# Hybrid conv/MoE step: one block shape with 32 rows of each of two experts, gate/up one block ahead, sorted pairs of experts

## The chip, the cores and the metric

The kernel runs on one core of a Trainium2 chip. The metric is the device time of one execution in microseconds (us). A core has five engines with their own instruction streams: TensorE (PE: matmuls, and transposes against an identity), VectorE (DVE), ScalarE (ACT), GpSimd (POOL) and SyncE (SP, which here only issues DMAs and waits). They meet through semaphores: an instruction may wait until a semaphore has reached a count. `bank0` to `bank7` are the eight PSUM banks, everything else named here lies in SBUF, except `h_rows`, `x_rows` and `y_rows`, which are the profile's names for scratch tensors in DRAM.

## The reference: what is computed

One decoder layer on 576 tokens (512 of a prompt, 64 of samples) of 1024 channels, all in float32. First a gated convolution mixer (not touched by the change), then a mixture of experts:

```
t   = RMSNorm(x)                                  # 576 x 1024
grp = argmax(t @ w_coarse + b)                    # 4 groups
top 2 of the 8 fine logits of that group          # so each token goes to 2 of 32 experts
out[token] += combine * (silu(t @ w_gate[e]) * (t @ w_up[e])) @ w_down[e]
y   = RMSNorm(x + out)
```

An expert's three matrices are 1 MB each (1024x256, 1024x256, 256x1024), 3.15 MB (10^6 bytes) in all, so the 32 experts are 100 MB, and each is read once from DRAM whatever the number of its tokens. How many tokens each expert gets follows from the inputs alone. For the inputs that are timed, experts 0 to 31 get

```
13 11 106 69 | 11 73 6 153 | 25 27 36 45 | 7 14 6 6 | 1 6 7 70 | 20 66 17 29 | 67 21 28 49 | 71 27 6 59
```

rows, 1152 in all.

## The kernel before: how the work is tiled and ordered

**Routing.** For each tile of 128 tokens (`NT` = 5 tiles, the last of 64) DVE selects the two experts (`select`), PE counts ranks within the expert by triangular matmuls (`rank`, L1498), and DVE turns ranks into a block number and a row in the block. `turns()` counts the tokens of the first two tiles and moves the pair of experts (2m, 2m+1), m >= 4, that has the fewest to the end of the order. At the end DVE holds `ends` (the block at which each expert ends), PE inverts the table with a one-hot matmul (L1550), and `gidx` / `sidx` say for each block which half rows to gather and scatter. `bound` holds the ends for the engines' registers.

**Blocks.** The experts are worked on in pairs, and rows in blocks of `T` = 64. Each pair has one block that is shared: 32 rows of the first expert and 32 of the second. What an expert has over 32 rows goes in blocks of 64 of its own, the first expert's ahead of the shared block and the second's behind it. So a pair with c0 and c1 rows has 1 + ceil((c0-32)/64) + ceil((c1-32)/64) blocks (a negative term counts as 0).

**One block** on PE is gate/up (`L1572` in a block of one expert: 16 matmuls of 64 rows by 256 columns; `L1577` in a shared block: 32 of 32 rows; the profile lists each float32 matmul of this kind twice), a dummy matmul `L1584`, four transposes `L1563` of the next block's gathered tokens (`tokens`), one transpose of the hidden values `L1587`, and the down product `L1597`. Beside it ACT does silu (`L722`) and copies the down product out of PSUM (`L726`), DVE multiplies (`L1256`, `s_hid`), copies the transposed hidden values (`L1258`, `s_hidT`), scales the next tokens (`L1249`, `s_xt`) and moves the gathered rows (`L1245`, `s_mv`), and POOL gathers (`L867`) two blocks ahead and scatters (`L897`) the block that is out. All of it is in program order on each engine; nothing is scheduled by a tool.

**Weights.** There are 8 slots for experts (`NSLOT`), so 4 rounds (`it` = 0 to 3). Slots 2m and 2m+1 hold the m-th pair of a round. The first round's experts are loaded while the mixer runs. From then on SP refills the slots in order: for each expert it waits until gate/up of the last block that used the slot is done (`s_gu`), issues gate (L440) and up (L440), waits until its last down product is done (`s_down`), and issues down (L438). A slot of a first expert is free after the shared block, one of a second expert at the end of the pair. After the last weights SP issues the loads of the residual (`xf`, L534) and `g_final` (L535) into slot memory, and once all scatters have landed those of the experts' results (L543).

**The end.** The results of the two experts of a token are read back from `y_rows`, weighted and added (DVE, and PE for two tiles), normalized and written out.

Of the kernel before, what the change touches and what calls it, by code (L numbers as in the profile page):

```python
# [6 lines left out]
P = 128  # L7
KC = D // P
SEQ = 512
NS, SL = 8, 8  # L10
NTOK = SEQ + NS * SL
# [16 lines left out]
T = 64  # L28
# [6 lines left out]
NBLK = NPAIR + NE + (2 * NTOK - NE * (T // 2 + 1)) // T  # L35
# [13 lines left out]
def build_step(nc, a, out):  # L49
# [8 lines left out]
    with ctx:  # L58
# [128 lines left out]
        bound = sb("bound", [1, 2 * NE + 4 + NPAIR], i32)  # L187

        PAIRS, ODD, LASTP, ORDER = NE + 1, NE + 2, NE + 3, NE + 4
        ENDS = ORDER + NE  # L190

        BITS = 6
        assert NBLK < 1 << BITS

        eps_rms, eps_ln = small[:, 60:61], small[:, 61:62]
        carry = sb("carry", [P, 6])[:, :]
        NCON = 18 + 2 * CC
# [113 lines left out]
        iota16, groupof = col(NPAIR), col(NE)  # L311

        expert_at, pair_at = iota32, iota16
# [5 lines left out]
        ends = col(NE)  # L319
# [3 lines left out]
        evens = col(NE)  # L323


        low32, sgn, sgnq, lower = col(2 * NT), col(2 * NT), col(2 * NT), col(2 * NT)
# [11 lines left out]
        pari, pairu = rtu[:, 0:2 * NT], rtu[:, 2 * NT:4 * NT]  # L338
        counti, nbi = coli(NE), coli(NE)
        nblki, pairi, parti, rowi = coli(1), coli(1), coli(1), coli(2 * NT)  # L340

# [15 lines left out]
        early = ps[7][:, 64 + 6 * NE:64 + 7 * NE]  # L357
# [28 lines left out]
        def _(sp):  # L386
# [123 lines left out]
            def turn(it, i):  # L510
                return (sp.value_load(bound[0:1, bass.ds(it * NSLOT + (i + ORDER), 1)], min_val=0, max_val=NE - 1),
                        sp.value_load(bound[0:1, bass.ds(it * NSLOT + (i + 1 - NSLOT), 1)], min_val=1, max_val=NBLK))

# [17 lines left out]
            left = sp.value_load(bound[0:1, NE - NSLOT + 1:NE - NSLOT + 2], min_val=1, max_val=NBLK)  # L531
# [24 lines left out]
        def _(act):  # L556
# [162 lines left out]
            def block_of(q, b):  # L719

                act.wait_ge(s_gu, q * 2 + (b + 1))
                nc.scalar.activation(sg_m, ps[1][:, 0:P], ACT.Silu).then_inc(s_silu, 1)  # L722
                act.wait_ge(s_down, q * 2 + (b + 1))
                if not isinstance(q, int):
                    act.wait_ge(s_ysc[b], q * 16)
# [956 lines left out]
```

## Time and profile before

| | us |
|---|---|
| median of three executions | 526.67 (526.08 to 532.02) |
| the profiled execution, its own time | 528.73 |
| span of that execution, first to last instruction | 527.0 |
| PE busy in the span | 478.6 (91%) |
| first gate/up starts | 273.07 |
| last down product ends | 494.9 |

All moments in the text are us from the start of the span of the profiled execution. Busy time says only that an instruction was in the engine; the chain of work that ended last says which engine's work set the end, and what an engine waited for is shown behind its idle time with the group it waited on.

### The profile page before, as it was taken

The page shows a single profiled execution, that of the slowest core. Times are in us where ns is not written, and L with a number is a line of the kernel's source. Part 1 is how long each engine was busy: PE and PEld are TensorE (multiplying, and loading weights), DVE is VectorE, ACT ScalarE, POOL GpSimd, SP SyncE. Part 2 cuts the span into 40 slices and gives each one's busy share as a digit, 9 for nine tenths or more (in the row PEclk, how much of TensorE's full clock was granted, in tenths as well). Part 3 has the DMA queues.
Part 4 walks back from the last instruction along what each step waited for, and adds up shares of the span by engine and source line. Part 5 has one row for each costly group of instructions (what it writes and reads, how often), then busy time and mean ns, then how long its engine had stood idle before and what let it go on. Part 6 is the DMA issues. An engine that isn't in the chain of part 4 may idle for free.

```text
span 527.0 us, 8895 instructions
## 1 busy us (share of the span) xinstructions
PE 478.6 (91%) x3289; PEld 283.4 (54%) x3290; DVE 237.0 (45%) x513; ACT 102.1 (19%) x209; POOL 183.0 (35%) x282
## 2 busy tenths in 40 slices
PE   6999999999999999999679999989979998979784
PEld 3887777777777645555434444444434444434331
DVE  4219999999993520335742222112212221122146
ACT  5130011011112523323511111111101111110213
POOL 3010915665575800101153434443433433442100
PEclk9989999999999999999789999999999999999998
DMA  8995005200000299936769999999999999999887
GB/s 328 319 391 157 0 2 206 113 2 0 1 1 1 87 363 424 393 146 205 308 227 420 416 410 390 418 418 419 415 387 419 422 418 419 395 414 420 268 280 260
DMA packets 43992, 146.01 MB, mean 277 GB/s; under 512 B 10240, under 2 KB 18448, under 8 KB 32697
## 3 DMA queue, kind: packets, MB, share of 16 engines
q1 hardware_dynamic: 37242, 131.06, 64.7%
q0 software_dynamic: 4960, 9.45, 4.8%
q10 hardware_dynamic: 1759, 5.06, 2.5%
q8 instruction: 22, 0.36, 0.3%
q14 instruction: 9, 0.07, 0.0%
HBM read 136.83 MB, written 15.53 MB: 289 GB/s over the span
## 4 chain that ended last, share of the span: by engine, by line
PE 77%; DMA 7%; issue 6%; DVE 4%; ACT 3%; SPq 1%; POOL 1%; DVEq 0%; POOLq 0%; ACTq 0%
PE bank L1374 27%; PE bank L1577 10%; PE bank L1457 10%; PE bank L1597 9%; PE bank L1572 9%; PE bank L1367 4%; DMA region_x<-in_w_up 2%; DMA region_w<-y_rows 2%; PE bank L1587 2%; PE bank L1483 2%; DVE region_m L1256 1%; DVE region_m L1258 1%; ACT region_m L722 1%; PE bank L1523 1%; DMA y_rows<-region_m,slast 1%
## 5 line engine op out<-in xcount | busy, mean ns | idle before, releaser
L1374 PE MATMUL bank<-region_m,region_w 128*128 128x256 f32 (+1 forms) x576 | 142.3, 409 | 0.0
L1374 PEld LDWEIGHTS bank<-region_m,region_w 128*128 128x128 f32 x576 | 110.3, 192 | 30.4 <-issue 0.6
L1256 DVE TENSOR_TENSOR region_m<-region_m,bank 128x128 f32<-128x128 f32 x30 | 8.7, 288 | 160.5 <-ACT region_m L722 160.5
L1457 PE MATMUL bank<-region_w,z 128*128 128x512 f32 x128 | 56.7, 595 | 0.2 <-ACT z L647 0.2
L1015 DVE SCALAR_TENSOR_TENSOR z<-region_m,z 128x512 f32<-128x512 f32 x60 | 48.7, 812 | 0.0
L1015 DVE SCALAR_TENSOR_TENSOR region_x<-region_m,region_x 128x512 f32<-128x512 f32 x56 | 45.9, 820 | 0.0
L1597 PE MATMUL bank<-region_w,region_m 128*32 128x512 f32 x272 | 40.3, 598 | 2.8 <-DVE region_m L1258 2.8
L807 POOL TENSOR_TENSOR region_m<-region_x 128x512 f32<-128x512 f32 x4 | 20.2, 5053 | 63.6 <-ACT region_m L601 32.4
L1457 PEld LDWEIGHTS bank<-region_w,z 128*128 128x128 f32 x128 | 23.8, 190 | 28.0 <-issue 26.3
L878 POOL COPY gcol<-gidx 128x1 uint32 (+1 forms) x30 | 5.4, 181 | 95.1 <-DVE region_m L1245 95.1
L589 ACT ACTIVATE region_x<-bank 128x256 f32<-128x256 f32 (+1 forms) x40 | 14.2, 407 | 123.6 <-PE bank L1374 104.0
L867 POOL DMA_INDIRECT region_x<-h_rows,gcol x30 | 31.7, 1055 | 15.1 <-issue 15.1
L726 ACT ACTIVATE region_m<-bank 128x512 f32<-128x512 f32 x30 | 17.9, 598 | 93.8 <-PE bank L1597 93.8
L1572 PE MATMUL bank<-region_w,z 128*64 128x256 f32 x288 | 34.6, 391 | 0.3 <-issue 0.3
L897 POOL DMA_INDIRECT y_rows<-region_m,scol x28 | 29.0, 1034 | 15.1 <-issue 15.1
L371 POOL TENSOR_SCALAR region_m<-region_m 128x128 f16<-128x128 f32 x7 | 6.0, 868 | 72.6 <-DVE region_m L1149 72.6
L1577 PE MATMUL bank<-region_w,z 128*32 128x256 f32 x384 | 30.6, 389 | 0.0
L722 ACT ACTIVATE region_m<-bank 128x128 f32<-128x128 f32 x30 | 8.3, 278 | 109.6 <-PE bank L1577 65.7
L1572 PEld LDWEIGHTS bank<-region_w,z 128*64 128x64 f32 x288 | 19.5, 134 | 18.7 <-issue 7.9
L1563 PE MATMUL bank<-ident,region_m 128*128 128x128 f32 x124 | 25.2, 286 | 2.4 <-DVE region_m L1245 2.4
L1597 PE MATMUL bank<-region_m 128*32 128x512 f32 x176 | 25.0, 598 | 1.5 <-DVE region_m L1258 1.5
L824 POOL TENSOR_TENSOR region_m<-region_x 128x512 f32<-128x512 f32 x4 | 11.4, 2842 | 31.0 <-ACT region_x L589 31.0
(240 smaller groups left out, 642.8 us busy)
## 6 DMA issues: line engine op xcount, KB each, us to landing
region_w<-in_w_down SPq DMA_DIRECT2D x16, 1024.0 KB
region_w<-in_w_gate SPq DMA_DIRECT2D x12, 1024.0 KB, 16.1
region_w<-in_w_up SPq DMA_DIRECT2D x12, 1024.0 KB
region_m<-in_w_down SPq DMA_DIRECT2D x12, 1024.0 KB
region_w<-in_w_in SPq DMA_DIRECT2D x4, 2048.0 KB, 18.7
region_m<-in_w_gate SPq DMA_DIRECT2D x8, 1024.0 KB
region_m<-in_w_up SPq DMA_DIRECT2D x8, 1024.0 KB
slot<-in_w_gate SPq DMA_DIRECT2D x4, 1024.0 KB
```

Source lines behind the costliest of these rows:

```text
L726: nc.scalar.activation(yblk[b], ps[3][:, :], ACT.Copy).then_inc(s_yc, 1)
L807: pool.tensor_tensor(ub[:, c, HB:HB + SEQ], sv[:, 0:SEQ], sg[:, 0:SEQ], ALU.mult)
L867: pool.indirect_dma_start(stage[b], None, h2_half, bass.IndirectOffsetOnAxis(ap=rows, axis=0), bounds_check=2 * NTOK - 1, oob_is_err=False ...
L897: pool.indirect_dma_start(y_half, bass.IndirectOffsetOnAxis(ap=rows, axis=0), yblk[b], None, bounds_check=4 * NTOK - 1, oob_is_err=False). ...
L1015: last[j % 2] = conv(nc.vector.scalar_tensor_tensor(out=acc[j % 2], in0=ub[:, c, j:j + SEQ], scalar=wB(c, j), in1=acc[j % 2], op0=ALU.mult ...
L1367: ins = mm(ps[2 * bank + j][:, at:at + hi - lo], sec[name][:, k, 0:P], hT[:, k, lo:hi], start=(k == 0), stop=(k == KC - 1))
L1374: ins = mm(ps[2 * bank + j][:, 0:LEN[j]], sec[name][:, k, c * P:(c + 1) * P], hT[:, k, CUT[j]], start=(k == 0), stop=(k == KC - 1))
L1457: ins = mm(ps[2 * (t % 2) + j][0:n, :], z[:, k, t * P:t * P + n], w_out_sb[:, k, j * 512:(j + 1) * 512], start=(k == order[0]), stop=(k == ...
L1563: ins = tr(ps[0][:, k * P:(k + 1) * P], xrow[:, k * P:(k + 1) * P], ident[:, :])
L1572: ins = mm(ps[1][h * T:(h + 1) * T, 0:2 * P].rearrange("p (w f) -> p w f", w=2), xT[:, k, :], wgu[halves[0]][:, :, k, h, :], start=(k == 0 ...
L1577: ins = mm(ps[1][r0:r0 + H, 0:2 * P].rearrange("p (w f) -> p w f", w=2), xT[:, k, half * H:(half + 1) * H], wgu[i][:, :, k, h, :], start=( ...
L1597: ins = mm(ps[3][quarter * H:(quarter + 1) * H, :], hidT[:, c * T + r0:c * T + r0 + H], wdn[halves[quarter % 2]][:, c, h * 512:(h + 1) * 512],
```

## The change

Every block now has one shape: 32 rows of each of the two experts of a pair. A pair with c0 and c1 rows has max(1, ceil(max(c0, c1)/32)) blocks, in all of which both experts' weights are used. On PE the blocks are software-pipelined: gate/up of block g+1 stands ahead of the transpose of block g's hidden values, of the next tokens' transposes and of block g's down product; ACT and DVE follow that order, and gate/up of a block waits for the product (`s_hid`) of the one before, as both use `bank1`. The dummy matmul L1584 is gone. `turns()` now counts the tokens of the first three tiles and sorts all of experts 8 to 31 by that count, largest first; neighbours in that order are the pairs. It moves from the fourth tile's turn to the fifth's, `rank` of the third tile four steps earlier on PE. SP waits for the end of a pair for both its slots, and issues gate and up of both experts, then down of both. Its order of slots is as before, and so are the loads before the loop.

```diff
-NBLK = NPAIR + NE + (2 * NTOK - NE * (T // 2 + 1)) // T
+HT = T // 2
+NBLK = (2 * NTOK + NPAIR * HT - 1) // HT
...
             with sp.Fori(1, NE // NSLOT) as it:
-                for i in range(NSLOT - 2):
-                    reload(i, *turn(it, i), range(3))
-                ends_of = [(i, *turn(it, i)) for i in range(NSLOT - 2, NSLOT)]
-                for which in (range(2), range(2, 3)):
-                    for i, e, last in ends_of:
-                        reload(i, e, last, which)
+                for i in range(0, NSLOT, 2):
+                    last = sp.value_load(bound[0:1, bass.ds(it * (NSLOT // 2) + (i // 2 + 1 - NSLOT // 2), 1)],
+                                         min_val=1, max_val=NBLK)
+                    pair = [(i + k, turn(it, i + k)) for k in range(2)]
+                    for which in (range(2), range(2, 3)):
+                        for j, e in pair:
+                            reload(j, e, last, which)
...
             act.wait_ge(s_x1d[NT - 1], 16)
-            for b in range(2):
-                block_of(0, b)
-            with act.Fori(1, pairs) as q:
-                for b in range(2):
-                    block_of(q, b)
+            silu(0, 0)
+            silu(0, 1)
+            y_out(0, 0)
+            silu(1, 0)
+            y_out(0, 1)
+            silu(1, 1)
+            y_out(1, 0)
+            with act.Fori(1, pairs - 1) as q:
+                silu(q + 1, 0)
+                y_out(q, 1)
+                silu(q + 1, 1)
+                y_out(q + 1, 0)
...
             def turns():
...
+                for r in range(0, NE - NSLOT, 8):
+                    link(nc.vector.max(top[:, r:r + 8], key))
+                    if r < NE - NSLOT - 8:
+                        link(nc.vector.scalar_tensor_tensor(out=key, in0=key, scalar=top[:, r + 7:r + 8], in1=key,
+                                                            op0=ALU.is_lt, op1=ALU.mult))
+                link(nc.vector.tensor_copy(topi, top))
+                link(nc.vector.tensor_scalar(topi, topi, NE - 1, None, ALU.bitwise_and))
+                link(nc.vector.tensor_copy(expert_at[:, NSLOT:NE], topi))
+                marks(0, NT - 2, s_again)
+                link(pairs_of(0, NT - 2))
+                placed(0, NT - 2).then_inc(s_place, NT - 2)
...
-                pe.wait_ge(s_mv, g + 2)
-                mm(ps[5][0:32, 0:1], onesb[:, 0:32], onesb[:, 0:1], start=True, stop=True)
-                tokens(0, KC // 4)
+            def next_tokens(g):
+                pe.wait_ge(s_mv, g + 1)
+                tokens(0, KC // 2).then_inc(s_xt_ps, 1)
+
+            def turn_hidden(g):
                 pe.wait_ge(s_hid, g + 1)
                 tr(ps[2][:, 0:P], hid, ident[:, :]).then_inc(s_hT_ps, 1)
-                tokens(KC // 4, KC // 2).then_inc(s_xt_ps, 1)
...
-            def pair(it, i, first, after, end):
+            def pair(it, i, first, end):
                 for part in range(2):
-                    pe.wait_ge(s_wexp[i][part], it * 16 + 16)
-                with pe.If(after > first + 1):
-                    with pe.Fori(first, after - 1) as g:
-                        block_of(g, (i, i), it)
-                for part in range(2):
-                    pe.wait_ge(s_wexp[i + 1][part], it * 16 + 16)
-                block_of(after - 1, (i, i + 1), it)
-                with pe.If(end > after):
-                    with pe.Fori(after, end) as g:
-                        block_of(g, (i + 1, i + 1), it)
+                    for half in range(2):
+                        pe.wait_ge(s_wexp[i + half][part], it * 16 + 16)
+                gate_up(first, i)
+                if isinstance(first, int):
+                    next_tokens(1)
+                else:
+                    turn_hidden(first - 1)
+                    next_tokens(first + 1)
+                    down(first - 1, (i - 2) % NSLOT, it if i else it - 1)
+                with pe.If(end > first + 1):
+                    with pe.Fori(first + 1, end) as g:
+                        gate_up(g, i)
+                        turn_hidden(g - 1)
+                        next_tokens(g + 1)
+                        down(g - 1, i, it)
```

How the order on the engines moves, at two places. PE, the shared block of the first round's second pair, before (`region_w` holds the two experts' weights, `bank` is PSUM, `ident` the identity of the transposes):

```order
L1577 MATMUL bank<-region_w,z 32x256 [waits s_xt,s_wexp3_up,s_wexp3_gate]
L1577 MATMUL bank<-region_w,z 32x256 x31
L1583 REGISTER_ALU
L1584 MATMUL bank<-onesb 32x1 [waits s_mv]
L1563 MATMUL bank<-ident,region_m 128x128 x2
L1587 MATMUL bank<-ident,region_m 128x128 [waits s_hid]
L1563 MATMUL bank<-ident,region_m 128x128 x2
L1597 MATMUL bank<-region_w,region_m 32x512 [waits s_wexp2_down,s_wexp3_down,s_yc,s_hidT]
L1597 MATMUL bank<-region_w,region_m 32x512 x7
```

The same place in the changed kernel, a later block of that pair (L1594 is gate/up, L1605 the transpose of the hidden values, L1581 the next tokens, L1615 down):

```order
L1594 MATMUL bank<-region_w,z 32x256 [waits s_hid,s_xt]
L1594 MATMUL bank<-region_w,z 32x256 x31
L1605 MATMUL bank<-ident,region_m 128x128 [waits s_hid]
L1600 REGISTER_ALU
L1581 MATMUL bank<-ident,region_m 128x128 [waits s_mv]
L1581 MATMUL bank<-ident,region_m 128x128 x3
L1615 MATMUL bank<-region_w,region_m 32x512 [waits s_wexp2_down,s_wexp3_down,s_yc,s_hidT]
L1615 MATMUL bank<-region_w,region_m 32x512 x7
```

The transpose and the down product are now those of the block before, so the product that they wait for is one gate/up old, and all four token transposes stand behind it.

SP, the refill of slots 2 and 3 in the loop over rounds, before (L511 and L512 load two registers for each expert):

```order
L440 ISA [waits s_gu]
L440 DMA region_w<-in_w_gate 128x2048
L440 DMA region_w<-in_w_up 128x2048
L438 DMA region_w<-in_w_down 128x2048 [waits s_down]
L511 ISA
L511 TENSOR_LOAD bound
L511 ISA x2
L512 ISA
L512 TENSOR_LOAD bound
L512 ISA x2
```

And in the changed kernel:

```order
L438 ISA [waits s_gu]
L438 DMA region_w<-in_w_gate 128x2048
L438 DMA region_w<-in_w_up 128x2048
L438 ISA [waits s_gu]
L438 DMA region_w<-in_w_gate 128x2048
L438 DMA region_w<-in_w_up 128x2048
L436 DMA region_w<-in_w_down 128x2048 [waits s_down] x2
```

Both waits for `s_gu` are now for the end of the pair, and the two down loads stand behind all four others.

## Rows read from the trace of the kernel before

**Rows 1.** The page: the span, and the chain that ended last by engine.

```profile
span 527.0 us, 8895 instructions
...
PE 77%; DMA 7%; issue 6%; DVE 4%; ACT 3%; SPq 1%; POOL 1%; DVEq 0%; POOLq 0%; ACTq 0%
```

**Rows 2.** DMA from 273 to 495 us: 40 slices in GB/s; queues: packets, MB, share.

```profile
GB/s 418 416 427 416 412 419 397 421 372 394 423 412 413 418 422 423 412 416 421 413 390 375 415 414 427 426 420 415 416 425 422 415 401 371 415 418 413 429 414 300
...
q1 hardware_dynamic: 16844, 81.54, 90.9%
q0 software_dynamic: 4640, 9.17, 10.9%
```

**Rows 3.** Chain that ended last, first gate/up and 291 to 298: start, us, what.

```profile
273.07 3.87 PE bank L1577 x64
...
291.46 0.29 ACT region_m L722
...
291.77 0.30 DVE region_m L1256
...
292.48 0.30 DVE region_m L1258
...
292.82 1.92 PE bank L1597 x16
294.75 3.69 PE bank L1577 x62
```

**Rows 4.** PE in order of time, one shared block: start, us, instructions, idle before.

```profile
461.99 1.92 PE L1597 MATMUL bank<-region_w,region_m 128*32 128x512 f32 x16 [0.17 <-DVE region_m L1258]
463.73 3.82 PE L1577 MATMUL bank<-region_w,z 128*32 128x256 f32 x64
...
468.28 0.33 PE L1587 MATMUL bank<-ident,region_m 128*128 128x128 f32 x1 [0.36 <-DVE region_m L1256]
468.44 0.38 PE L1563 MATMUL bank<-ident,region_m 128*128 128x128 f32 x2
468.99 1.92 PE L1597 MATMUL bank<-region_w,region_m 128*32 128x512 f32 x16 [0.17 <-DVE region_m L1258]
```

**Rows 5.** SP in order of time: the issues of weights and residual.

```profile
277.55 0.36 SPq L440 DMA_DIRECT2D slot<-in_w_gate  x1
...
298.60 0.33 SPq L440 DMA_DIRECT2D region_w<-in_w_gate  x1
...
433.82 20.08 SPq L440 DMA_DIRECT2D z<-in_w_up  x1
...
468.12 11.08 SPq L534 DMA_DIRECT2D slot<-x_rows  x5
```

**Rows 6.** Waits, 255 to 527 us: who for whom, us, times, longest.

```profile
POOL gcol L878 <- DVE region_m L1245: 95.1, 29, 5.8
...
ACT region_m L722 <- PE bank L1577: 65.7, 16, 11.1
ACT region_m L722 <- PE bank L1572: 43.9, 14, 3.4
```

**Rows 7.** Windows: busy of PE, PEld, DVE, ACT, POOL; PEclk, DMA share, GB/s.

```profile
257.00:264.00 7.00, 3.32 (x24) 1.58 (x23) 6.05 (x39) 5.25 (x8) 0.95 (x1) 0.52 1.00 398
...
267.00:267.50 0.50, 0.50 (x3) 0.20 (x2) 0.43 (x4) 0.00 (x0) 0.00 (x0) 0.53 0.00 0
...
470.00:475.00 5.00, 2.31 (x37) 0.94 (x30) 0.00 (x0) 0.60 (x1) 2.85 (x6) 1.00 1.00 419
...
523.00:523.50 0.50, 0.00 (x0) 0.00 (x0) 0.50 (x2) 0.00 (x0) 0.00 (x0) 0.97 1.08 229
```

**Rows 8.** DVE in order of time: the wait for ranks ahead of the fifth tile.

```profile
252.18 0.22 DVE L1127 TENSOR_TENSOR region_m<-region_m,bank 128x64 f32<-128x64 f32 x1 [4.43 <-PE bank L1498]
```

**Rows 9.** In order of time: the last down product and the last scatter.

```profile
492.99 1.92 PE L1597 MATMUL bank<-region_m 128*32 128x512 f32 x16 [0.17 <-DVE region_m L1258]
...
496.36 0.99 POOL L897 DMA_INDIRECT y_rows<-region_m,slast  x1 [0.51 <-issue]
```

More of the change, by code:

```diff
@@ L318, in build_step @@
         sbase = col(NE)
-        ends = col(NE)
+        zeros, of_pair, starts = col(NPAIR + 1), col(NPAIR + 1), col(NPAIR + 1)
+        key = col(NE - NSLOT)
         pick2 = col(4 * NE)
@@ L1093, in turns @@
                 nc.vector.tensor_copy(bound[0:1, ORDER:ORDER + NE], expert_at[0:1, :])
-                for t in range(2):
-                    marks(t, s_again)
-                pairs_of(0, 2)
             def select(t):
@@ L1263, in _ @@
             move(0, 1)
-            with nc.vector.Fori(0, pairs) as q:
+            for b in range(2):
+                block_of(0, b)
+            with nc.vector.Fori(1, pairs) as q:
                 for b in range(2):
                     block_of(q, b)
-                    tokens_out(q * 2 + (b + 2))
-                    move(q + 1, b)
+            turned(pairs * 2)
             with nc.vector.If(odd > 0):
-                block_of(pairs, 0)
+                hidden(pairs, 0)
+                turned(pairs * 2 + 1)
             dve.wait_ge(s_w12, 1)
@@ L1488, in rank @@
                 pe.wait_ge(s_mask, t + 1)
[L1489 to L1493 removed]
+                if t == NT - 2:
+                    pe.wait_ge(s_again, 1)
+                if t == NT - 3:
+                    for u in range(t + 1):
+                        mm(early, onesb[:, :], maskb[:, u * NE:(u + 1) * NE], start=(u == 0), stop=(u == t))
                 for v in ((t, NT) if t == NT - 1 else (t,)):
@@ L1620, in pair_of @@
-            def pair_of(it, i, first=None):
-                if first is None:
-                    first = pe.value_load(bound[0:1, bass.ds(it * NSLOT + i, 1)], min_val=0, max_val=NBLK - 1)
-                after, end = bounds(bound[0:1, bass.ds(it * (NSLOT // 2) + (i // 2 + ENDS), 1)])
-                pair(it, i, first, after, end)
-                return end
+                    for half in range(2):
+                        pe.wait_ge(s_wexp[i + half][part], it * 16 + 16)
+                gate_up(first, i)
@@ L1628, in _, with end_of @@
             keep_busy(10)
             pe.wait_ge(s_tab, 1)
-            round0 = [bounds(bound[0:1, ENDS + m:ENDS + m + 1]) for m in range(NSLOT // 2)]
+            def end_of(at):
+                return pe.value_load(at, min_val=1, max_val=NBLK)
+            round0 = [end_of(bound[0:1, m + 1:m + 2]) for m in range(NSLOT // 2)]
             pe.wait_ge(s_mv, 1)
             tokens(0, KC // 2).then_inc(s_xt_ps, 1)
-            end = 0
-            for m, (after, last) in enumerate(round0):
-                pair(0, 2 * m, end, after, last)
-                end = last
+            first = 0
@@ L1638, in _ @@
+            for m, end in enumerate(round0):
+                pair(0, 2 * m, first, end)
+                first = end
             with pe.Fori(1, NE // NSLOT) as it:
-                end = None
+                first = end_of(bound[0:1, bass.ds(it * (NSLOT // 2), 1)])
                 for i in range(0, NSLOT, 2):
-                    end = pair_of(it, i, end)
+                    end = end_of(bound[0:1, bass.ds(it * (NSLOT // 2) + (i // 2 + 1), 1)])
+                    pair(it, i, first, end)
+                    first = end
@@ L1643, in _ @@
+            blocks = end_of(bound[0:1, NPAIR:NPAIR + 1])
+            turn_hidden(blocks - 1)
+            down(blocks - 1, NSLOT - 2, NE // NSLOT - 1)
             for i, t in enumerate(BY_PE):
```

181 lines of the change are left out of this document (83 added, 98 removed).

## The prediction

> **What bounds the kernel now.** Read the page first: the span is 527.0 us, and PE has 77% of the chain that ended last [rows 1]. That view names one engine for each moment and hides a second one that is just as late. So read the DMA in slices over the expert stage next: from 273 us, where the first gate/up starts [rows 3], to 492 us no slice falls below 371 GB/s, and the mean of the 39 full slices is 412 GB/s [rows 2]. The stage has two bounds at once: PE goes from block to block with no long wait, and the DMA is never idle.
>
> When do the weights end? The SP queue moved 81.54 MB there and the gathers and scatters 9.17 MB [rows 2]. The 24 experts of rounds 1 to 3 are 75.5 MB, the residual and `g_final`, issued last [rows 5], 2.9 MB, so 3.1 MB were still outstanding at 273 us. 87.8 MB at 412 GB/s are 213 us: the last weight lands at about **486 us**, and the last down product ends at 494.9 us [rows 9]. Behind it stand a copy, the last scatter at 496.36 us [rows 9] and the reading back; the change leaves this tail of 32 us alone.
>
> The DMA stays full because slots come free early. SP issued the refill of slot 0 at 277.55 us, and that of slot 2 at 298.60 us, after 4 blocks [rows 5]. Later the queue is so full that one issue takes 20.08 us [rows 5].
>
> **The change part by part.**
>
> *Number of blocks.* ACT waited for gate/up 16 times in shared and 14 times in other blocks: 30 blocks [rows 6], which the rule and the counts of tokens give too (1, 4, 2, 3 for the first round's pairs). By the new rule the first round has 1, 4, 3, 5. Counting the first 384 tokens and sorting gives the pairs (19,28) (24,21) (27,11) (31,23) (10,29) (26,9) (8,25) (20,13) (22,14) (12,15) (30,18) (17,16) with 3, 3, 2, 2, 2, 1, 1, 1, 1, 1, 1, 1 blocks: 32 in all. Pairs end after blocks 1, 5, 8, 13, 16, 19, 21, 23, 25 and then one by one to 32.
>
> *Length of a block.* A shared block takes 5.26 us from the start of gate/up to that of down (463.73 to 468.99) and 1.74 us from there to the next gate/up (461.99 to 463.73): 7.0 us [rows 4]. In it PE stands still for silu 0.29, product 0.30 and copy 0.30 us [rows 3]. With gate/up of the next block ahead, all three lie under it. What is left is PE's own work: gate/up 3.7 us [rows 3], five transposes at 0.16 us (468.28 to 468.44) [rows 4], down 1.74 us: 6.2 us. The waits that are left are short: down comes 0.71 us after the transpose of the hidden values [rows 4], and four token transposes fill 0.64 us of it; DVE's scaling of the next tokens has the 1.74 us of down to hide in. I take **6.3 us**. The bounds are 6.2 us (nothing else shows) and 7.0 us (the new order hides nothing, or instruction supply takes it back). The dummy matmul goes into this sum at nothing.
>
> *POOL.* A scatter now waits for the down product of its block, which stands behind the next gate/up, and the next gather is queued behind that scatter. POOL idled 95.1 us over 29 gathers, 3.3 us a block [rows 6], and a gathered block is wanted two blocks later. I put 0 on it; if it shows, it is part of the 7.0 us bound.
>
> *Releases, the term that decides.* The slots of a pair are refilled from the end of its gate/up on. Block 1 ends its gate/up at 276.9 us (273.07 + 3.87) [rows 3], block 2 at about 281.5, as its tokens can't be transposed ahead, and block n at 281.5 + 6.3 (n - 2). The fourth pair of round 0 holds slots 6 and 7 until block 13: 350.8 us. What can the DMA have done by then? The 3.1 MB outstanding, three pairs of 6.29 MB, and 442 routed rows of these 13 blocks at 8.2 KB for gather and scatter (9.17 MB over 1152 rows [rows 2]), 3.6 MB: 25.6 MB or 62.1 us of the 77.7 us. **15.6 us of DMA time are lost**, spread over the waits for blocks 5, 8 and 13. The load of the eighth pair then takes 15.3 us, 2.8 us for rows and about 1 us to get going again; it ends at 369.9 us, when block 16 has just freed the next slots (369.7). The ninth ends at 387.9, block 19 at 388.6: 0.7 us lost and 1 us to start. From the tenth on the queue is never empty. Lost in all: 15.6 + 1 + 0.7 + 1 = **18.3 us**. With 6.2 us a block it is 16.8, with 7.0 us 30.4.
>
> The restart I took at 1 us, an estimate. The Trainium skill (DMA: Bandwidth & Descriptors, Anatomy of one DMA) gives a fixed cost of about 2.0 us per DMA; no row here shows one alone, and by it the sum would be up to 2 us longer.
>
> Since everything behind is bound by the DMA, the weights end at 486 + 18.3 = 504.3 us. PE, at 6.3 us a block, would reach block 28's end near 449 us, and from there on waits for every pair, one block each: pairs arrive 15.3 us apart, the work between is 6.3 us.
>
> *The end.* The last two parts to land are down weights (5.1 us), so the last gate/up weight lands at 499.2, usable at some 500.2 us. Then follow gate/up 3.7, transposes 0.8, the down product of block 31 1.74, a register load that I put at 1 (0 to 2), the transpose of the hidden values and its copy 0.71, down 1.92 [rows 4, 9]: 9.9 us, to 510.1 us.
>
> *The clock.* Before the last blocks PE now stands still for about 9 us each. In this trace a wait of 2.7 us in 470 to 475 us left the granted clock at 1.00 (2.4 GHz); but in the routing, where PE was busy for 3.32 of 7 us, it was 0.52 on average, it came back only in 267.0 to 267.5 us, and at the end it began to fall in 523.0 to 523.5 us, a stretch without a matmul [rows 7]. So I expect the last blocks to start at 1.2 GHz. In the earlier ones that fits into the wait. In the last one gate/up costs up to 3.7 us more and what follows up to 4.4: bounds 0 and 8, I take **4.5 us** (gate/up and a little): 514.6 us.
>
> The Trainium skill (TensorE: Matmul & The Clock Gate, HAM oscillation) tells of a kernel whose waits for loads lowered the clock before every group of matmuls; by that rule this term stays, and without it the sum is 4.5 us less. The fall at 523 us agrees, but no row here has a block behind a long wait.
>
> *Routing.* The sort, with the marks of three tiles, is 14 instructions on DVE in a row, some 0.2 to 0.35 us each, 3.3 us, about what the old `turns()` took one tile earlier. It lies ahead of the fifth tile, where DVE waits 4.43 us for the ranks [rows 8], and `rank` is four steps earlier, so that wait shrinks and holds most of it; four small instructions per tile are gone, two are added for tiles 3 and 4. I take 0, bounds -1 and +2 us.
>
> **The sum.** The last down product ends at 514.6 instead of 494.9 us: +19.7 us. The profiled execution took 528.73 us for a span of 527.0 [rows 1]; that makes 548.4. The median of the three executions was 2.1 us under it: **546.4 us**, 3.7% more.
>
> **The rivals.**
>
> 1. *The chain is right, and PE's saving is all there is.* 30 blocks of 7.0 us become 32 of 6.3: 210 to 201.6 us, so about 518 us; with the idle pieces around pairs gone too, 515 us, faster by 2%. For it speaks PE's 77% [rows 1]; against it that the DMA was full until 492 us [rows 2], so that a faster PE only waits for weights. It decides only if weights could land before 486 us. Chance 0.03.
>
> 2. *Loads keep pace.* If the slots came free in time, the weights would still end at 486 us, and with 5.9 us from there to the last down product the time would be 526.7 - 3 = 523.6 us, no difference. That takes 13 blocks in 62 us, 4.8 us each, under PE's own 6.2. A milder form, where about half of the loss is made up (early loads overlap more than I think, or rows move for less), gives 530 to 537 us. Chance 0.13.
>
> 3. *The clock holds*, as in the 2.7 us wait [rows 7]: 542 us. Chance 0.20.
>
> 4. *Blocks stay near 7.0 us*, because instruction supply, the scatter order on POOL or the copy of the hidden values stall PE: 30.4 us lost instead of 18.3, so 558.5 us. Chance 0.14.
>
> 5. *The forecast*, starved early, bound by weights late, at low clock: 0.50.
>
> **How the numbers follow.** 546.4 us is the likeliest case. Rivals 3 and 4 reach from 542 to 558.5, and with the bounds of period and clock (16.8 us lost and no clock term give 540.4) the slow cases lie in 540 to 560. The range 535 to 559 leaves out the first rival, most of the second and the worst ends of the fourth, under 2 in 10. A difference of about 2% is what a measurement of this kernel can tell from none: that is 516.1 and 537.2 us. Faster has 0.03, within 2% 0.13, slower 0.84.
>
> **What would show it.** Right: 32 blocks (ACT's silu 32 times); a distance of gate/up to gate/up near 6.3 us in the first round's fourth pair; DMA slices well under 400 GB/s between 318 and 351 us, and full ones after 390; SP waiting for gate/up of block 13 for over 8 us; PE waits of about 9 us for weights ahead of each of the last three or four blocks, and PEclk at 0.5 there; the last weight near 504 us. Wrong: a DMA that is full all along (then the slots were free in time), a period near 7.0 us, or a last gate/up at full clock. If the time is under 530 us, the count of lost DMA time is what failed.

## The result and the profile after

The changed kernel takes **546.04 us** (median of 4 executions, 545.54 to 547.65), the kernel before, on the same chip, 528.17 (526.08 to 532.02). The ratio is 1.034, with a 95% interval of 1.027 to 1.041: slower. The forecast was 546.4 us with a range of 535 to 559. The profiled execution took 545.83 us for a span of 544.0. An execution more than 1.5% above the fastest of its kernel counts as slow here, and the intervals leave such executions out.

The page of the changed kernel, with the lines that answer to [rows 1]:

```profile
span 544.0 us, 10128 instructions
...
PE 79%; DMA 7%; SPq 6%; issue 4%; ACT 2%; DVE 1%; POOL 1%; DVEq 0%; POOLq 0%; ACTq 0%
```

PE's share of the chain has grown, from 77 to 79%, and PE is not what got slower. Read alone, this view would again point at the wrong engine. The DMA slices from 273 to 515 us say more (each is 6.05 us long, columns as in [rows 2]):

```profile
GB/s 404 427 417 418 209 379 412 362 270 401 410 135 59 308 421 385 313 400 423 342 391 422 390 379 419 420 418 424 414 421 417 424 420 384 385 419 417 428 419 303
DMA packets 21904, 90.81 MB, mean 375 GB/s; under 512 B 3615, under 2 KB 9759, under 8 KB 13003
```

The bytes are those of before. What is new are the holes: the fifth slice, the ninth, and above all the twelfth and thirteenth, 340 to 352 us, at 135 and 59 GB/s. Before, no slice of the stage fell below 371 [rows 2]. From the 21st slice on no slice but the last, in which the loads run out, falls below 379.

SP in order of time shows what the DMA lacked. Each line is the first load for a pair of slots:

```profile
278.34 0.37 SPq L438 DMA_DIRECT2D slot<-in_w_gate  x1
...
302.25 0.34 SPq L438 DMA_DIRECT2D region_w<-in_w_gate  x1
...
320.95 0.63 SPq L438 DMA_DIRECT2D z<-in_w_gate  x1
...
351.93 0.34 SPq L438 DMA_DIRECT2D region_m<-in_w_gate  x1
...
371.50 0.35 SPq L438 DMA_DIRECT2D slot<-in_w_gate  x1
...
390.12 0.34 SPq L438 DMA_DIRECT2D region_w<-in_w_gate  x1
```

These are the ends of blocks 1, 5, 8, 13, 16 and 19, just as the rule of the pairs' ends gives them. Before, the first gate of slots 6 and 7 was issued at 327.28 us. In SP's waits the group of `s_gu` (L438) says the same; the longest of them, 19.4 us, ends at block 13. The second line is the group of `s_down` (who for whom, us, times, longest):

```profile
SPq L438 <- PE bank L1594: 58.0, 8, 19.4
SPq L436 <- PE bank L1615: 52.7, 9, 7.6
```

PE itself is faster, as forecast. Two gate/ups in a row of the first round's fourth pair, PE in order of time:

```profile
323.13 3.81 PE L1594 MATMUL bank<-region_m,z 128*32 128x256 f32 x64
326.86 0.33 PE L1605 MATMUL bank<-ident,region_m 128*128 128x128 f32 x1
327.03 0.60 PE L1581 MATMUL bank<-ident,region_m 128*128 128x128 f32 x4
...
329.32 3.83 PE L1594 MATMUL bank<-region_m,z 128*32 128x256 f32 x64
```

The distance is 6.19 us instead of 7.0 [rows 4], and no line has an idle time in brackets: silu, product and copy lie under matmuls. And at the end PE stands still ahead of each of the last four pairs (the number in brackets is the idle time and what ended it):

```profile
458.05 0.60 PE L1594 MATMUL bank<-slot,z 128*32 128x256 f32 x1 [8.44 <-DMA region_w<-in_w_up]
...
473.34 5.96 PE L1594 MATMUL bank<-region_w,z 128*32 128x256 f32 x64 [7.37 <-DMA region_w<-in_w_up]
...
489.73 0.60 PE L1594 MATMUL bank<-z 128*32 128x256 f32 x1 [7.86 <-DMA region_x<-in_w_up]
...
504.61 5.70 PE L1594 MATMUL bank<-region_m,z 128*32 128x256 f32 x64 [6.02 <-DMA region_m<-in_w_up]
...
513.72 1.92 PE L1615 MATMUL bank<-region_m 128*32 128x512 f32 x16 [0.58 <-DVE region_m L1266]
```

Gate/up takes 5.1 to 6.3 us there instead of 3.8. The windows name the reason (columns as in [rows 7], the clock behind ACT's and POOL's):

```profile
485.00:490.00 5.00, 0.27 (x4) 0.23 (x8) 0.00 (x0) 0.00 (x0) 1.25 (x2) 0.50 1.02 422
490.00:495.00 5.00, 5.00 (x52) 2.65 (x48) 0.00 (x0) 0.00 (x0) 0.00 (x0) 0.50 1.01 413
505.00:510.00 5.00, 5.00 (x64) 2.69 (x56) 0.00 (x0) 0.00 (x0) 0.00 (x0) 0.64 1.01 415
```

The granted clock is 0.50 (1.2 GHz) behind a wait of 7.86 us in which PE did nothing, and it comes back in the course of the gate/up.

### The profile page after: what moved, and what is told of

Read it like the earlier page. It is cut to its first block, busy times and chain, and to the rows that moved or that the text cites. A ratio compares the mean times of both kernels' runs of the same rounds, so it can differ in the third digit from the quotient of the medians.

```text
span 544.0 us, 10128 instructions
## 1 busy us (share of the span) xinstructions
PE 488.9 (90%) x3878; PEld 291.0 (53%) x3879; DVE 235.6 (43%) x489; ACT 103.7 (19%) x213; POOL 189.0 (35%) x293
## 4 chain that ended last, share of the span: by engine, by line
PE 79%; DMA 7%; SPq 6%; issue 4%; ACT 2%; DVE 1%; POOL 1%; DVEq 0%; POOLq 0%; ACTq 0%
PE bank L1392 26%; PE bank L1594 20%; PE bank L1475 10%; PE bank L1615 10%; SPq L438 4%; PE bank L1385 3%; PE bank L1581 2%; DMA region_x<-in_w_up 2%; DMA region_w<-y_rows 2%; PE bank L1541 1%; PE bank L1605 1%; PE bank L1501 1%; DMA h_rows<-region_m 1%; PE bank L1376 1%; PE bank L1673 1%
## 5 line engine op out<-in xcount | busy, mean ns | idle before, releaser
L1266 DVE COPY region_m<-bank 128x128 f32<-128x128 f32 x32 | 9.4, 292 | 181.7 <-PE bank L1605 181.7
L1594 PE MATMUL bank<-region_w,z 128*32 128x256 f32 x800 | 66.6, 412 | 8.2 <-DMA region_w<-in_w_up 7.4
L1594 PEld LDWEIGHTS bank<-region_w,z 128*32 128x32 f32 x800 | 33.5, 115 | 27.6 <-issue 14.5
L1615 PE MATMUL bank<-region_w,region_m 128*32 128x512 f32 x256 | 44.2, 599 | 0.0
L823 POOL TENSOR_TENSOR region_m<-region_x 128x512 f32<-128x512 f32 x4 | 21.0, 5247 | 62.5 <-ACT region_m L599 32.1
L1594 PE MATMUL bank<-region_m,z 128*32 128x256 f32 x576 | 36.2, 404 | 6.0 <-DMA region_m<-in_w_up 6.0
L902 POOL COPY scol<-sidx 128x1 uint32 x30 | 5.3, 177 | 99.9 <-ACT region_m L728 99.9
L1594 PE MATMUL bank<-slot,z 128*32 128x256 f32 x224 | 30.1, 424 | 10.8 <-DMA region_w<-in_w_up 8.4
L1594 PE MATMUL bank<-z 128*32 128x256 f32 x224 | 29.2, 416 | 7.9 <-DMA region_x<-in_w_up 7.9
L1594 PEld LDWEIGHTS bank<-region_m,z 128*32 128x32 f32 x576 | 19.5, 113 | 24.9 <-issue 13.4
L1615 PE MATMUL bank<-region_m 128*32 128x512 f32 x200 | 30.7, 598 | 1.0 <-DVE region_m L1266 0.6
## 6 DMA issues: line engine op xcount, KB each, us to landing
region_m<-in_w_down SPq DMA_DIRECT2D x12, 1024.0 KB, 18.3
region_w<-in_w_in SPq DMA_DIRECT2D x4, 2048.0 KB, 18.8
```

Of the source, the lines that this page charges most:

```text
L823: pool.tensor_tensor(ub[:, c, HB:HB + SEQ], sv[:, 0:SEQ], sg[:, 0:SEQ], ALU.mult)
L1594: ins = mm(ps[1][r0:r0 + H, 0:2 * P].rearrange("p (w f) -> p w f", w=2), xT[:, k, half * H:(half + 1) * H], wgu[i + half][:, :, k, h, :], ...
L1615: ins = mm(ps[3][quarter * H:(quarter + 1) * H, :], hidT[:, c * T + r0:c * T + r0 + H], wdn[i + quarter % 2][:, c, h * 512:(h + 1) * 512], ...
```

## The experiments

The theory is the forecast's: PE's saving is real but unusable, since the slots of a pair come free only at its end, the DMA runs dry in the first rounds, and everything behind is bound by weights. The first rival says that PE's work sets the time; the second that the weights are late for another reason, and what PE does early is hidden. The first group of experiments leaves the weights' bytes alone and moves PE's time or the releases. Medians are compared with 546.0 us of the changed kernel and with the kernel before, run beside each. Ratios are to the latter. The changed kernel itself was not run again beside them, and its own interval is some 4 us wide to either side, so a difference of 1 to 3 us from its 546.0 is not told from none.

**Delay in the first round, and delay at the end.** Four dummy matmuls behind each block of the first round; in another kernel twelve behind each block of the last two rounds.

```diff
+            def slower(it):
+                if isinstance(it, int):
+                    keep_busy(4)
...
                     down(first - 1, (i - 2) % NSLOT, it if i else it - 1)
+                    slower(it)
...
                         down(g - 1, i, it)
+                        slower(it)
```

and in the other kernel

```diff
+                if not isinstance(it, int):
+                    with pe.If(it > 1):
+                        keep_busy(12)
```

> The changed kernel (546.0 us), with four dummy matmuls of 512 columns behind each block's down product in the first round alone. Ten such matmuls took 2.33 us, so four add 0.93 us to a block of PE; eleven of them stand ahead of gate/up of block 13, 10.3 us in all. The theory of late releases (the weights are issued only when a pair ends, the DMA idles until block 13, and all that comes behind is bound by the DMA) expects nearly all of it in the time: 554 to 557 us, and gate of slots 6 issued near 362 us instead of 351.9. The rival that the weights are late for another reason (a slower DMA, or the order of the loads) expects no more than 1 or 2 us, since PE waits for weights for 30 us later on: 546 to 548.

> The changed kernel (546.0 us), with twelve dummy matmuls of 512 columns (2.8 us) behind each block's down product in the last two rounds alone, nine times, 25 us of PE in all. The theory of late releases expects them to vanish in the waits for weights (8.4, 7.4, 7.9 and 6.0 us) but for the one that stands between the last gate/up and the last down product: 547 to 550 us. The rival that PE's work sets the end, as the chain's 79% of PE would have it, expects the larger part of 25 us: 560 to 571.

Measured: 558.0 us (1.060, 1.056 to 1.064) and 547.4 us (1.039, 1.035 to 1.043). So 10.3 us of PE in the first round cost 12 us, a little over the expected 8 to 11, and 25 us of PE in the last two rounds cost 1.4, which is within the noise of none. The profiled execution of the first took 556.2 us, 10.4 more than that of the changed kernel; in it the gate of slots 6 is issued 9.2 us later, and the last pair's weights come 10.7 us later (515.34 for 504.61):

```profile
361.16 0.34 SPq L438 DMA_DIRECT2D region_m<-in_w_gate  x1
```

In the second the dummies lie in the waits: the gate/up that waited 7.37 us now waits 0.42 us and starts where it did, within 0.8 us:

```profile
472.56 3.85 PE L1594 MATMUL bank<-region_w,z 128*32 128x256 f32 x64 [0.42 <-DMA region_w<-in_w_up]
```

Both rivals fall here. A microsecond of PE counts ahead of block 13, and behind block 23 nearly nothing of it does.

**The order of the releases alone.** The same experts in the same pairs, but in the opposite order in the first round's slots.

```diff
+FIRST = (6, 7, 4, 5, 2, 3, 0, 1)
...
             def load_part(i, part, e):
+                e = FIRST[e] if isinstance(e, int) else e
...
+            for i in range(NSLOT):
+                if FIRST[i] != i:
+                    link(nc.vector.memset(expert_at[:, i:i + 1], float(FIRST[i])))
```

> The changed kernel (546.0 us), with the four pairs of experts of the first round in the opposite order: 6,7 then 4,5 then 2,3 then 0,1, so that they have 5, 3, 4, 1 blocks instead of 1, 4, 3, 5. The same 32 blocks, the same bytes, the same matmuls. The first slots come free only after block 5, near 300 us instead of 278. Late releases: the DMA has nothing to load from about 282 to 300 us, and the fourth pair's wait is shorter; 22 us idle instead of 14, so about 7 to 10 us more: 553 to 556. Rival, PE's work or the number of blocks decides: no difference, 545 to 547.

Measured: 554.15 us (1.052, 1.048 to 1.056), 8.1 us more for the same work. The DMA from 273 us on has its longest hole where the five blocks of the first pair are, in the second to the sixth slice:

```profile
GB/s 417 299 26 51 45 327 411 416 334 407 410 107 241 387 410 416 421 420 416 419 418 421 410 413 363 413 418 419 423 420 422 424 418 418 410 358 424 414 428 423
```

**Early releases.** With the same three edits and another table, `(0, 1, 4, 6, 5, 3, 2, 7)`, the first round has 1, 1, 3, 5 blocks.

> The changed kernel (546.0 us), with the eight experts of the first round placed in its slots by their counts (0,1 then 4,6 then 5,3 then 2,7), a table written for these inputs. Its pairs have 1, 1, 3, 5 blocks, 10 instead of 13, and release after blocks 1, 2, 5 and 10, near 278, 283, 302 and 333 us. By then the DMA has had 62 us of work to do from 273 us on, so by the theory of late releases it never runs dry: the weights end near 488 instead of 507 us, and the time falls by about 17 us to 528 to 530, which is before's, since both are then bound by the DMA. The low clock before the last blocks stays. A rival by which PE's three blocks less count alone expects 546 - 18.6 = 527.4, hardly to be told apart by the time, but a PE that still waits 6 to 9 us ahead of the last pairs, and a DMA without a gap, decide for the first.

Measured: 529.95 us, a ratio of 1.003 (0.999 to 1.007): the whole loss is gone, and nothing is won. This table also takes three blocks away, 29 instead of 32, some 18.6 us of PE, so the time alone can't tell fewer blocks from earlier releases. The trace can. No slice falls below 326 GB/s before the last weights are in, and PE still waits for weights at the end, so the work that went away is not what bounded it (the same views as above):

```profile
GB/s 416 422 421 417 419 417 417 377 390 419 399 416 423 326 395 417 354 330 421 412 367 411 421 416 424 419 418 418 423 421 416 352 417 426 427 423 372 181 259 351
```

```profile
457.74 5.73 PE L1599 MATMUL bank<-region_w,z 128*32 128x256 f32 x64 [5.83 <-DMA region_w<-in_w_up]
474.25 0.61 PE L1599 MATMUL bank<-z 128*32 128x256 f32 x1 [8.22 <-DMA region_x<-in_w_up]
489.05 5.50 PE L1599 MATMUL bank<-region_m,z 128*32 128x256 f32 x64 [6.24 <-DMA region_m<-in_w_up]
```

The last weights come 15.6 us earlier than in the changed kernel (489.05 for 504.61). The table is written for these inputs, so this kernel shows a cause and is no general repair.

**What PE alone would take.** The loads of rounds 1 to 3 cut to a quarter, in both kernels; the rest of a slot keeps the first round's weights.

```diff
+                if not isinstance(e, int):
+                    if part == 2:
+                        sp.dma_start(slot_dn[i][:, 0:2 * F], rows[:, 0:2 * F]).then_inc(s_wexp[i][part], 16)
+                    else:
+                        sp.dma_start(slot_gu[i][:, part, 0:2, :], rows.rearrange("p (k n) -> p k n", k=KC)[:, 0:2, :])\
+                          .then_inc(s_wexp[i][part], 16)
```

> The kernel before (526.7 us) with the loads of rounds 1 to 3 cut to a quarter (2 of the 8 chunks of gate and up, 512 of 2048 columns of down); the rest of the slot keeps the first round's weights. PE does the same work. It shows what the kernel would take if PE and not the weights bounded it: 30 blocks of 7.0 to 7.1 us from 273 us, last down product near 487, so 518 to 521 us.

> The changed kernel (546.0 us) with the same cut of the loads to a quarter. 32 blocks of 6.2 us and the round transitions: last down product near 477 us instead of 515.6, so 507 to 510 us, some 11 us less than the kernel before with the same cut. If both hold, the change makes PE's part faster by what was forecast, and the 38 us between are all waits for weights. Rival: PE's blocks are not really shorter in sum, and this stays above 518.

Measured: 521.25 us (520.44 to 522.78) and 509.71 us (506.90 to 512.08). PE waits for no weights in either from 273 us on. The last down products start at these moments, first in the kernel before, then in the changed one:

```profile
488.34 1.92 PE L1603 MATMUL bank<-region_m 128*32 128x512 f32 x16 [0.17 <-DVE region_m L1264]
```

```profile
477.39 1.92 PE L1621 MATMUL bank<-region_m 128*32 128x512 f32 x16 [0.58 <-DVE region_m L1272]
```

The change makes PE's part 11 us shorter, in spite of two blocks more. The kernel before sits 7 us above its PE bound; the changed kernel sits 36 us above its own.

**The pipelining taken back.** Block shape, sort and releases stay; in a block all engines work in the old order.

```diff
-                gate_up(first, i)
...
+                def block_of(g):
+                    gate_up(g, i)
+                    next_tokens(g + 1)
+                    turn_hidden(g)
+                    down(g, i, it)
```

> The changed kernel (546.0 us) with gate/up no longer ahead of the down product of the block before: the order of work in a block is the old one (gate/up, next tokens, transpose of the hidden values, down), on ACT and DVE too. Block shape, sorting and releases stay. Period 7.0 us instead of 6.2. Late releases: block 13 ends its gate/up some 9 us later, and the DMA loses that and a few us for blocks 16 to 21: 556 to 562 us. Rival, PE hidden behind weights: 546 to 548.

Measured: 556.6 us (1.052, 1.045 to 1.059). The period is back at 7.0 us (329.67 to 336.68), slots 6 are refilled from 361.74 us on, 9.8 us later, and the last pair's weights come 13.0 us later (517.61). So pipelining is worth some 10.6 us to the new block shape, and it comes through earlier weights; the new shape without it would have cost 28 us. No run takes the other cause of late releases apart, the longer stay of a pair and the release of both slots at its end: before, the gates of slots 6 and 7 were issued at 327.28 and 341.01 us, after at 351.93 and 352.94.

**The sort taken back.**

```diff
-                link(nc.vector.scalar_tensor_tensor(out=key, in0=early[:, NSLOT:NE], scalar=float(NE), in1=iota32[:, NSLOT:NE],
-                                                    op0=ALU.mult, op1=ALU.add))
+                link(nc.vector.tensor_scalar(key, iota32[:, NSLOT:NE], -float(NE - 1), float(NE * (NE - 1)), ALU.mult, ALU.add))
```

> The changed kernel (546.0 us) with the key of the sort replaced by the place itself, so that experts 8 to 31 stay in their order and their pairs have 1, 2, 1, 1, 1, 3, 3, 1, 3, 2, 3, 2 blocks: 36 in all instead of 32. The sort's own instructions stay. The first 13 blocks are the same, so the larger part of the DMA's idle time is too; the release after block 16 is now after block 14, which gives back 1 to 3 us, and the last pair has two blocks, 6.2 us more behind the last weights, less of a low clock. 548 to 552 us. If PE's work set the end, four blocks more would cost 25 us: 571.

Measured: 548.3 us (1.044, 1.038 to 1.050). Four blocks more, 25 us of PE, cost 2.3 us. With them the profile puts one wait of PE down to weights, of 1.91 us, and PE and DMA end together. The same trace has waits of another kind, for which the profile names no releaser, the longest at the start of a round:

```profile
396.24 0.61 PE L1593 MATMUL bank<-slot,z 128*32 128x256 f32 x1 [4.80 <-issue]
```

**The low clock.** Dummy matmuls ahead of the wait for weights in the last round, first 24, then 30 of them; and 22 instead of 10 ahead of the first block.

```diff
             def pair(it, i, first, end):
+                if not isinstance(it, int):
+                    with pe.If(it > 2):
+                        keep_busy(24)
```

> The changed kernel (546.0 us), with 24 dummy matmuls of 512 columns (5.6 us at full clock) ahead of the wait for weights in the last round's four pairs, where PE stands still for 6.0 to 8.4 us. In the last pair gate/up took 5.70 us at the low clock instead of 3.7. If the low clock follows from the wait, gate/up there takes 3.7 us and the time is 2.0 us less: 544.0. If the dummies don't keep the clock, or a gap of 1 to 3 us behind them is enough to lower it, 546; if they run at the low clock themselves and outlast the waits, 1 to 4 us more. The prediction had put 4.5 us on this.

> The changed kernel (546.0 us), with 30 dummy matmuls of 512 columns ahead of the wait for weights in the last round instead of the 24 of the run before. With 24, gate/up of the last pair still began 3.48 us behind the last dummy and took 5.46 us at a falling clock, while the one that began 2.91 us behind took its full-clock time. 30 last 6.7 us and leave gaps of 0.2 to 2.3 us. If the low clock is what the last pair's gate/up costs, it takes 3.7 us now and the time is 1.5 to 2.0 us less: 544.0 to 544.5. If something else stretches it, it stays near 5.5 us and 546.

> The changed kernel (546.0 us), with 22 instead of 10 dummy matmuls ahead of the first block. In the changed kernel these ended at 267.0 us, the clock fell, and gate/up of block 1 took 5.81 us instead of before's 3.87. With 12 more (2.8 us) the clock should hold. Late releases: gate/up of block 13 ends 1.9 us earlier, the DMA idles as much less, and the whole is 1.9 us shorter: 544.1. Rival, what happens before the wait for the last weights is hidden: 546.0.

Measured: 546.3 us with 24 (1.037, 1.034 to 1.040), 549.3 with 30 (1.042, 1.039 to 1.046), 546.1 with the 22 at the start (1.035, 1.030 to 1.041): none is faster. The reasons differ. With 24, a gap was left behind the dummies; PE of that kernel, the third and fourth of the last pairs:

```profile
489.25 0.39 PE L1594 MATMUL bank<-z 128*32 128x256 f32 x1 [2.91 <-DMA region_x<-in_w_up]
...
504.42 5.46 PE L1594 MATMUL bank<-region_m,z 128*32 128x256 f32 x64 [3.48 <-DMA region_m<-in_w_up]
```

Behind a gap of 2.91 us the single matmul took 0.39 us, behind one of 3.48 us the whole gate/up took 5.46: the only one of the four that lies on the path still ran at the low clock. With 30, the only execution with a trace is one of 566.8 us, 17 us above the median. Its page and PE:

```profile
q8 instruction: 39, 0.64, 0.5%
```

```profile
424.86 0.61 PE L1594 MATMUL bank<-slot,z 128*32 128x256 f32 x1 [8.55 <-issue]
450.08 0.60 PE L1594 MATMUL bank<-z 128*32 128x256 f32 x1 [4.41 <-issue]
478.92 8.68 PE L1348 MATMUL bank<-ident,onesb 128*128 128x512 bf16 x30 [11.49 <-issue]
```

The queue that loads instructions had 39 packets; it had 20 in the changed kernel and 21 with 24 dummies. PE waits 8.55, 4.41 and 11.49 us there without a named releaser, the first two in rounds in which no dummies run; from 467 to 479 us three packets of that queue moved beside 391 GB/s in all. That reads as if PE waited for its own code, which is longer by six matmuls in each of the loop's four pairs and has to pass the same DMA engines as the weights. It is argued and not shown: no run changes the code's size alone, and `not_sorted` has its wait of 4.80 us with 20 packets. Of the seven others one took 568.2 us and six 547.4 to 550.6; without a trace of them, their 1 to 4 us over the kernel with 24 dummies stay unexplained. With 22 at the start the first gate/up is at full clock, slots 6 are refilled at 350.34 us (1.6 earlier), the last weights come at 503.87 (0.7 earlier), and the gate/up behind them took 6.47 us instead of 5.70. The expected 1.9 us did not come: what was gained in front went into the low clock at the end. With executions from 541 to 551 us this one stays inconclusive.

**All repairs in one kernel.** The table of `first_round_sorted`, 22 dummies at the start, and the last round written out behind the loop with another order:

```diff
+                last_round = isinstance(it, int) and it > 0
+                if last_round:
+                    turn_hidden(first - 1)
+                    down(first - 1, (i - 2) % NSLOT, it if i else it - 1)
+                    keep_busy(30)
```

> The first round's experts placed by their counts (530.0 us alone), the 22 dummies ahead of the first block, and the last round written out behind the loop: there the transpose and the down product of the block before stand ahead of the wait for the next pair's weights instead of behind its gate/up, with 30 dummies behind them. From 530.0: 2.0 us for the clock of the last gate/up, 2 to 3 us for the transposes, the down product (1.74 us) and a register load that no longer stand between the last weights and the last down product; nothing for the first block, as the DMA has no gap that it could shorten. 525 to 526.5 us, against 527 to 528.7 for the kernel before. If the transfers behind the last weights (residual, g_final) set the end instead, no gain: 529 to 530.

Measured: 532.1 us (1.007, 1.003 to 1.011) instead of the expected 525 to 526.5, and 2 us above the table alone, where the two intervals overlap. PE from the third of the last pairs on:

```profile
479.33 0.47 PE L1610 MATMUL bank<-ident,region_m 128*128 128x128 f32 x1 [2.56 <-issue]
480.18 1.06 PE L1620 MATMUL bank<-region_w,region_m 128*32 128x512 f32 x1 [0.38 <-DVE region_m L1271]
...
483.75 7.53 PE L1353 MATMUL bank<-ident,onesb 128*128 128x512 bf16 x30
491.21 3.83 PE L1599 MATMUL bank<-region_m,z 128*32 128x256 f32 x64
```

The gate/up did run at full clock, but it began 2.2 us later than in the kernel with the table alone (489.05), and not behind a load. First came a wait of 2.56 us without a named releaser (27 packets in the instruction queue), in which the granted clock fell from 1.00 to 0.50, then a down product at that clock (1.06 us a matmul instead of 0.6) and dummies that ran partly at it. The last scatter is issued 1.5 us earlier all the same (499.92 for 501.40), and the reading back then took longer. No version here that loads all weights beats the kernel before. The 2.0 us that the low clock costs the last gate/up are read from its duration; no run has won them back.

## Why the prediction was right

The mechanism held: late releases, a DMA that runs dry in the first rounds, weights that bound all that follows. That the sum comes within 0.4 us of the median is luck, as three of its terms missed by 3.4 to 4.4 us each and cancelled.

**What bounds the kernel.** Confirmed: PE and DMA were both at their limit before. With weights cut, the kernel before gains 7 us; with PE shortened and the DMA kept full, nothing is gained (529.95).

**Blocks and period.** 32 blocks were forecast, and ACT's silu ran 32 times; 6.3 us a block, measured 6.2 (the lower bound). The waits on POOL did not show.

**Releases.** The forecast had block 13 end its gate/up at 350.8 us, and blocks 16 and 19 at 369.7 and 388.6. The refills are issued at 351.93, 371.50 and 390.12; the 1.1 to 1.8 us more are mostly the first gate/up, which took 5.81 us instead of 3.87 [rows 3]. That low clock was not foreseen: the ten dummies ahead of it ended at 267.0 us, 2.1 us earlier than before. Lost DMA time was put at 18.3 us. The loads of the residual, issued behind all weights, measure it: issued from 468.12 us on before [rows 5] and landed 22.9 us later in the median, issued from 485.49 us on after and landed 24.3 us later. The DMA issues of the two kernels, the last number being the median from issue to landing:

```profile
slot<-x_rows SPq DMA_DIRECT2D x4, 512.0 KB, 22.9
```

```profile
slot<-x_rows SPq DMA_DIRECT2D x4, 512.0 KB, 24.3
```

Reckoned from the first issue with these medians, that is 491.0 and 509.8 us: **18.8 us**. No run isolates the restart of the DMA, for which the sum has 1 us twice. The section of the Trainium skill that the prediction names beside it (DMA: Bandwidth & Descriptors, Anatomy of one DMA) describes transfers issued by GpSimd, and these loads are issued by SP.

**Three terms were mis-sized and cancelled.** The last gate/up weight was forecast usable at 500.2 us and came at 504.6 (+4.4): its base, weights that end at 486 us in the kernel before, was some 4 us early, as the residual's landing at 491.0 shows. The prediction counted all of the residual and `g_final` among what had moved by 495 us, and called the DMA full until 492; but the 39 full slices end at 489.5 us, and SP's queue moved 0.91 MB more from 495 to 501.6 us, which is 2.2 of these 4 us (queues of the kernel before in that window):

```profile
q1 hardware_dynamic: 260, 0.91, 42.1%
```

The rest of the base's error is open. From there to the end of the last down product 9.9 + 4.5 us were forecast and 11.0 measured (-3.4), of which 9.0 by full-clock durations and 2.0 from the low clock, as that ended within gate/up (5.70 us for 3.7). And the tail behind the last down product, "left alone" at 32 us, took 28.4 (515.6 to 544.0, -3.7). The last scatter is 3.0 us of it: it needed 5.14 us to land before, where the DMA still moved 226 GB/s when it was issued and 37 when it landed, and 2.19 us after, at 43 to 29 GB/s. That the remaining loads held it up is argued from these rates (the chain of each kernel):

```profile
496.36 5.14 DMA y_rows<-region_m,slast
```

```profile
517.16 2.19 DMA y_rows<-region_m,slast
```

4.4 - 3.4 - 3.7 is -2.7, which is, but for rounding, the 2.6 us between the 548.4 us forecast for the profiled execution and its 545.83.

**The clock.** The term has the right cause and was too large: 2.0 instead of 4.5 us. The Trainium skill (TensorE: Matmul & The Clock Gate, HAM oscillation) tells of the clock falling in waits for loads before each group; this trace agrees, with 0.50 behind each of the four waits of 6 us and more. Its rival, that the clock holds (542 us), is excluded by the same rows.

**Routing.** Put at 0, measured -0.7 us to the first gate/up (272.36 for 273.07), and +1.9 in it by the clock.

**The rivals.** "PE's saving is all there is" needs weights before 486 us; the cut loads show what it would then give (509.7 us, with fewer bytes to load). "Loads keep pace" is what `first_round_sorted` built. "Blocks stay near 7.0" was priced at 558.5 us; the blocks took 6.2, and `not_ahead`, built with 7.0, measured 556.6.

## What to carry to other kernels

Where work and loads are both at their limit, the time is set by when buffers come free, and a step that makes the work denser may hold them longer: write down for each buffer the block after which it is released, and add up the bytes the DMA has left at that moment. Put short users of buffers ahead of long ones; the first round's 13 blocks in the opposite order cost 8 us here, and the sort of only the later rounds could not reach the one round in which it mattered. And dummy matmuls against a low clock won nothing in four kernels here: look in the trace at the granted clock of the work that they are to help, and at new waits of PE for which no releaser is named.

## What the runs showed of the hardware

- PE idled without a named releaser for 8.55, 4.41 and 11.49 us in the execution of 566.8 us with 30 dummies (39 packets in the instruction queue), for 2.56 us in `all_three` (27 packets), and for 4.80 us in `not_sorted` (20 packets, as in the changed kernel). So the number of these packets alone does not tell whether such a wait comes.
- The clock behind gaps: the matmuls behind gaps of 2.41 and 2.69 us (before), 1.54 and 2.91 us (24 dummies) ran at 2.4 GHz, those behind 3.35 us (after), 3.48, 3.68 and all longer ones at 1.2. Between them the length of the gap alone does not decide. The gap of 2.56 us in `all_three` had 1.2 GHz behind it, and four token transposes took 1.11 us behind 2.98 us in `small_loads_before` but 0.66 us behind 3.04 us in `slow_first_round`.
- A scatter of the same size took 5.14 us to land while the DMA moved 226 falling to 37 GB/s and 2.19 us at 43 to 29 GB/s.
